# One rope product for each pair of heads, and the odd head's three query items in slots 4, 6 and 8, in a TensorE-bound diffusion block

## The reference

```python
q = (rmsnorm(h @ w_dq, q_norm) @ w_uq).reshape(b, n, N_HEADS, QK_NOPE + QK_ROPE)   # 128 + 64 features a head
qr_l = axial_rope(qr_l, ang_row, ang_col)                  # the 64 rope features of each head are rotated
s = (einsum("bqhd,bkhd->bhqk", q_nope, k_nope)
     + einsum("bqhr,bkr->bhqk", q_rope, k_rope))
p = softmax(s * ATTN_SCALE)
```

## Time and profile before

| what | value |
|---|---|
| median of 3 runs | 2343.84 us |
| lowest and highest of them | 2341.87 and 2344.94 us |
| span of the profiled execution, first to last instruction | 2340.9 us |
| TensorE (PE) busy | 2316.5 us, 99% |
| VectorE (DVE) busy | 1706.3 us, 73% |
| ScalarE (ACT) busy | 807.6 us, 34% |
| GpSimd (POOL) busy | 152.5 us, 7% |
| scores, attention loop and last pass | about 103 to 540 us of the span |
| the odd heads' R products | 123 us, and 230, 338 and 447 us in the loop |

### The profile page before, as it was taken

The page is one execution under the profiler, slowest core; times in us unless marked ns, Lnnn a source line. Parts: engine busy times, 40 slices in busy tenths (PEclk is TensorE's granted clock), DMA queues, the critical chain, the costliest instruction groups (busy, mean ns, idle before and its releaser), DMA issues.

```text
span 2340.9 us, 29301 instructions
## 1 busy us (share of the span) xinstructions
PE 2316.5 (99%) x11037; PEld 1916.2 (82%) x11037; DVE 1706.3 (73%) x2568; ACT 807.6 (34%) x1301; POOL 152.5 (7%) x114
## 2 busy tenths in 40 slices
PE   8999999999999999999999999999999999999998
PEld 5888888888888888888888888888888888888887
DVE  5778788786688888888886764264897777777776
ACT  6355455563443222222223511111532222222224
POOL 0121221100300000000001200000200000000002
PEclk9999999999999999999999999999999999999999
DMA  7101111123112333333332020120111111111112
GB/s 298 34 25 53 43 52 43 43 74 125 64 36 72 108 108 108 108 101 107 108 100 90 19 72 28 45 72 28 45 45 54 46 47 53 54 47 54 54 38 89
DMA packets 49208, 163.35 MB, mean 70 GB/s; under 512 B 5312, under 2 KB 8768, under 8 KB 48960
## 3 DMA queue, kind: packets, MB, share of 16 engines
q1 hardware_dynamic: 49088, 161.72, 20.6%
HBM read 157.51 MB, written 4.19 MB: 69 GB/s over the span
## 4 chain that ended last, share of the span: by engine, by line
PE 94%; DVE 4%; DMA 1%; ACT 0%; issue 0%; SPq 0%; POOL 0%; DVEq 0%; ACTq 0%
PE ps L628 26%; PE ps L630 26%; PE ps L629 26%; PE ps L1106 3%; PE ps L1040 2%; PE ps L1044 2%; PE ps L1042 2%; PE ps L1041 2%; PE ps L1045 2%; PE ps L1085 1%; PE ps L1087 1%; PE ps L1086 1%; DMA ada_ring<-ada_pe 1%; PE ps L876 1%; PE ps L894 0%
## 5 line engine op out<-in xcount | busy, mean ns | idle before, releaser
L2220 DVE SCALAR_TENSOR_TENSOR x<-ps,mods,x 128x512 f32<-128x512 f32 x440 | 322.5, 748 | 145.1 <-PE ps L630 125.6
L628 PE MATMUL ps<-g_hi,w_hi 128*128 128x512 f32 (+1 forms) x848 | 327.5, 386 | 0.1
L630 PE MATMUL ps<-g_hi,w_lo 128*128 128x512 f32 (+1 forms) x848 | 326.5, 385 | 0.0
L629 PE MATMUL ps<-g_lo,w_hi 128*128 128x512 f32 (+1 forms) x848 | 326.5, 385 | 0.0
L628 PE MATMUL ps<-h_hi,op_hi 128*128 128x512 f32 x640 | 249.2, 389 | 0.0
L630 PE MATMUL ps<-h_hi,op_lo 128*128 128x512 f32 x640 | 249.0, 389 | 0.0
L1752 ACT CAST op_hi<-rq 128x512 fp32r<-128x512 f32 x240 | 146.7, 621 | 234.2 <-PE ps L630 228.9
L1763 ACT ACTIVATE g_full<-g_full 128x512 f32<-128x512 f32 x80 | 50.6, 633 | 491.1 <-DVE g_full L2572 491.1
L628 PE MATMUL ps<-h_hi,w_hi 128*128 128x512 f32 x512 | 200.6, 392 | 1.6 <-DVE h_lo L2450 1.5
L630 PE MATMUL ps<-h_hi,w_lo 128*128 128x512 f32 x512 | 199.3, 389 | 0.0
L629 PE MATMUL ps<-h_lo,w_hi 128*128 128x512 f32 x512 | 199.2, 389 | 0.0
(11 more groups left out here) (365 smaller groups left out, 4567.9 us busy)
## 6 DMA issues: line engine op xcount, KB each, us to landing
rq<-stream SPq DMA_DIRECT2D x80, 512.0 KB, 3.6
mod_raw_f<-ada_rows SPq DMA_DIRECT2D x48, 512.0 KB, 3.6
raw<-stream SPq DMA_DIRECT2D x46, 512.0 KB, 4.1
w_lo_f<-stream SPq DMA_DIRECT2D x46, 512.0 KB, 4.4
mod_raw<-ada_rows SPq DMA_DIRECT2D x32, 512.0 KB, 3.5
ada_ring<-ada_pe SPq DMA_DIRECT2D x16, 512.0 KB, 11.4
x<-x_t SPq DMA_DIRECT2D x8, 512.0 KB, 7.4
hraw<-head_w SPq DMA_DIRECT2D x8, 384.0 KB, 3.1
```

Source lines behind the costliest of these rows:

```text
L628: nc.tensor.matmul(out, w[0][wi], a[0][ai], start=start, stop=False)
L629: nc.tensor.matmul(out, w[0][wi], a[1][ai], start=False, stop=False)
L630: return nc.tensor.matmul(out, w[1][wi], a[0][ai], start=False, stop=stop)
L2220: nc.vector.scalar_tensor_tensor(out=x[:, m, HALF[half]], in0=ps[:, out_bank(d, m), :], scalar=mods[:, gate + m:gate + m + 1], in1=x[:, m, ...
```

## The change

The rope weights of the even and the odd head of a pair are put side by side in place of the even head's own twice, so one pair of R items gives the even head's 64 features in rows 0 to 63 and the odd head's in rows 64 to 127. The odd head (`pair_leads` false) has no R items; its W, Q0 and Q1 stand in slots 4, 6 and 8. In `FIRST_ITEMS` the two R items of head 1 are gone. `rope_done` writes the rounded part from and to the head's own rows, and the remainder to the other rows; for the odd head it waits for no rotation, since `qsb` still holds it. For the even head `hraw` arrives in four DMAs: two of them fetch 64 columns (256 bytes) twice a partition, from this head and from the next. For the odd head only the first 384 columns are split by `HW`.

```diff
+FOLLOW_AT = {4: ("W", 0), 6: ("Q", 0), 8: ("Q", 1)}
...
-            if 4 <= k <= 8:
-                kind, half = QUERY_STAGE[k - 4]
-                out.append((kind, gb, half))
+            if pair_leads(gb) and 4 <= k <= 8:
+                out.append((QUERY_STAGE[k - 4][0], gb, QUERY_STAGE[k - 4][1]))
+            if not pair_leads(gb) and k in FOLLOW_AT:
+                out.append((FOLLOW_AT[k][0], gb, FOLLOW_AT[k][1]))
...
+def pair_leads(gb):
+    return head_parity(gb) == 0
...
-                  ("W", -1, 0), ("F", -3, 1), ("M", 0, 3), ("R", -1, 0), ("R", -1, 1), ("X", 0, 3), ("Q", -1, 0),
+                  ("W", -1, 0), ("F", -3, 1), ("M", 0, 3), ("X", 0, 3), ("Q", -1, 0),
...
+        def pair_in(own, other):
+            sp.dma_start(hraw[:, 0:3 * P], own[:, 0:3 * P]).then_inc(in_head, 16)
+            sp.dma_start(rope_of(hraw)[:, :, 0:ROPE], rope_of(own)[:, :, 0:ROPE]).then_inc(in_head, 16)
+            sp.dma_start(rope_of(hraw)[:, :, ROPE:P], rope_of(other)[:, :, ROPE:P]).then_inc(in_head, 16)
+            sp.dma_start(hraw[:, HW:HW + P], own[:, HW:HW + P]).then_inc(in_head, 16)
+            C.add("uv_l")
...
-            C.add("q_rot")
-            dve.wait_ge(q_rot, C.at("q_rot"))
-            q = qr[par]
-            own(nc.vector.tensor_copy(q[:, HALF[k]], qsb[k][:]))
-            low = q[64:128, HALF[k]]
-            last = lo_part(low, qsb[k][64:128, :], low)
+            if par == 0:
+                C.add("q_rot")
+                dve.wait_ge(q_rot, C.at("q_rot"))
+            rows = (slice(0, ROPE), slice(ROPE, P))
+            full, top, low = qsb[k][rows[par], :], qr[par][rows[par], HALF[k]], qr[par][rows[1 - par], HALF[k]]
+            own(nc.vector.tensor_copy(top, full))
+            last = lo_part(low, full, top)
...
+            used = slice(0, HW if pair_leads(gb) else 3 * P)
+            copy(hw_hi[:, used], hraw[:, used]).then_inc(hw_h, 1)
```

More of the change, by code:

```diff
@@ L714, in _, with rope_of @@
         sp.dma_start(tab[:].rearrange("p a t -> p (a t)"), rope).then_inc(in_tab, 16)
+        def rope_of(t):
+            return t[:, 3 * P:HW].rearrange("p (q n) -> p q n", n=P)
+        def pair_in(own, other):
[4 more added lines that the diff above has]
+            C.add("uv_l")
         def head_in(n):
-            sp.wait_ge(uv_l, C.at("uv_l"))
             sp.dma_start(hraw[:], tile_of(head_w, n)).then_inc(in_head, 16)
@@ L727, in _ @@
         sp.wait_ge(pj, 4)
-        sp.dma_start(hraw[:], head_w[0]).then_inc(in_head, 16)
-        C.add("uv_l")
+        pair_in(head_w[0], head_w[1])
         sp.wait_ge(pj, 6)
@@ L734, in _ @@
         C.add("mod_p", 2)
+        sp.wait_ge(uv_l, C.at("uv_l"))
         head_in(1)
@@ L739, in _ @@
             for j in range(2):
-                head_in(i * 2 + (2 + j))
+                if j == 0:
+                    sp.wait_ge(uv_l, C.at("uv_l"))
+                    sp.sem_inc(wait_end, 1)
+                    pair_in(tile_of(head_w, i * 2 + 2), tile_of(head_w, i * 2 + 3))
+                else:
+                    sp.wait_ge(uv_l, C.at("uv_l"))
+                    sp.sem_inc(wait_end, 1)
+                    head_in(i * 2 + 3)
                 for k in range(4):
@@ L1184, in _ @@
         with pe.Fori(0, PASSES) as i:
-            C.enter(i, {"ra": RING_PASS, "rd": RING_PASS - 12, "ex": 16, "q_ready": 2, "hw_l": 2, "uv_l": 2, "ri": 4,
+            C.enter(i, {"ra": RING_PASS, "rd": RING_PASS - 10, "ex": 16, "q_ready": 2, "hw_l": 2, "uv_l": 2, "ri": 4,
                         "ol_l": 4})
@@ L1572, in ring_out @@
                 if k == 0:
-                    C.add("q_ready")
+                    C.add("q_ready", 2)
                 copy(qsb[k][:], ps[:, bank, :]).then_inc(ra, 1)
@@ L1599, in prepare, with head_hi @@
                 split_head(n, half)
-        def head_hi():
-            C.add("in_head", 16)
+        def head_hi(gb):
+            C.add("in_head", 64 if pair_leads(gb) else 16)
             act.wait_ge(in_head, C.at("in_head"))
-            copy(hw_hi[:], hraw[:, 0:HW]).then_inc(hw_h, 1)
+            used = slice(0, HW if pair_leads(gb) else 3 * P)
+            copy(hw_hi[:, used], hraw[:, used]).then_inc(hw_h, 1)
         def value_hi(par):
@@ L1625, in item @@
             elif kind == "HW":
-                head_hi()
+                head_hi(gb)
             elif kind == "UV":
@@ L1702, in _ @@
         with act.Fori(0, passes) as i:
-            C.enter(i, {"rg": RING_PASS, "mx": 16, "in_head": 32, "q_ready": 2, "pv": 40,
+            C.enter(i, {"rg": RING_PASS, "mx": 16, "in_head": 80, "q_ready": 2, "pv": 40,
                         "mod_p": 8, "mod_out": 1})
@@ L2249, in mods_ready, with head_lo @@
             scale_vec(2, mods[:, mod_col(0, SCALE2):mod_col(0, SCALE2) + KD], 1).then_inc(sv_set, 1)
-        def head_lo():
+        def head_lo(gb):
             C.add("hw_h")
             dve.wait_ge(hw_h, C.at("hw_h"))
-            lo_part(hw_lo[:], hraw[:, 0:HW], hw_hi[:]).then_inc(hw_l, 1)
+            used = slice(0, HW if pair_leads(gb) else 3 * P)
+            lo_part(hw_lo[:, used], hraw[:, used], hw_hi[:, used]).then_inc(hw_l, 1)
         def value_lo(par):
@@ L2310, in item @@
             elif kind == "HW":
-                head_lo()
+                head_lo(gb)
             elif kind == "UV":
@@ L2427, in _ @@
         with dve.Fori(0, passes) as i:
-            C.enter(i, {"ra": RING_PASS, "s_mm": 16, "ex": 16, "hw_h": 2, "uv_h": 2, "q_rot": 4, "pv": 40, "ol_r": 4,
+            C.enter(i, {"ra": RING_PASS, "s_mm": 16, "ex": 16, "hw_h": 2, "uv_h": 2, "q_rot": 2, "pv": 40, "ol_r": 4,
                         "v": 16 + 4 + 4 + 6 + 8, "in_mod0": 64, "in_mod1": 64, "mod_out": 1})
@@ L2993, in _ @@
         with pool.Fori(0, passes) as i:
-            C.enter(i, {"q_sh": 4, "gp": 8})
+            C.enter(i, {"q_sh": 2, "gp": 4})
             for gb in range(4):
```

## The result

| | before | after |
|---|---|---|
| median of the first comparison (4 runs each) | 2344.16 us | 2331.07 us |
| median of a second one (9 and 5 runs) | 2342.25 us | 2331.05 us |
| span of the profiled execution | 2340.9 us | 2329.4 us |

The ratio is 0.9946 in the first comparison, 95% interval 0.9933 to 0.9959, and 0.9952 (0.9938 to 0.9965) in the second: faster by 0.5%, 11 to 13 us. The forecast was 9.7 us and 2334.1 us. The measured median lies 0.4 us under the low end of the stated range, 2331.5.

The account below looks back on a forecast made before the run. PE without gaps was taken as the bound: 8.2 us in the loop plus 1.55 before it made 9.7 us, taken from the 2343.84 us median, giving 2334.1 us; range 2331.5 to 2338.3 us.

Parts of the forecast that it names:

- What bounds the kernel: Whole kernel: PE busy 2316.5 of 2340.9 us and without gaps in the loop, so time comes almost only from PE work.
- 2.73 us for a head's R items in the loop: Group 3 of three passes: two R items removed, at six starts of 0.228 us each; 8.2 us in all.
- The walk of group 3: New order on old durations, slots 5 to 8: no PE wait, nearest margin about 0.3 us, at Q1 for T9's `pt_lo`.
- near 26.2: Sign in the loop: group 3 becomes 2.7 us shorter, to near 26.2 us.
- mod_row at 1.22 us, since POOL is idle: Second `mod_row` of group 3 on DVE takes 1.22 us; with 1.94, PE would wait 0.4 us a pass, 1.2 in all.
- Before the loop, 1.55 us instead of 3.0: Head 1's R items: saving held to DVE's idle 1.55 us ahead of the row maximum; bounds nothing and 3.0 us.
- The two remainders do not come sooner with the change: Before the loop, DVE: Q0's and Q1's remainders stay put, since Q0's rounding on ACT stands behind an exponential that does not move.
- relief that is worth nothing: ACT copies, DVE shuffles, POOL operations and the split cut from 640 to 384 columns: beside gapless PE, worth nothing by themselves.
- Rival A: Before the loop nothing is held back: all 3.0 us saved, 11.2 us in all, 2332.7 us; chance 0.10.
- The load, F and the wider operands at nothing: Four-piece load covered (17.7 us for even heads; upper bound 0.6 us for the first), `rope_done` on 64 partitions: no cost.
- `hraw` lands within 5 us: Sign for the head weight loads: `hraw` lands within 5 us.
- Nothing given back behind attention: After attention PE is the chain again and loads are issued by progress, so none of the saving is lost there.

Follow-up runs that it names:

- the products alone, in the loop: Changed kernel with the odd head's twelve rope products put back on PE in each loop pass, result overwritten: 2340.35 us against 2342.56 before, ratio 0.9989.

## Why the prediction was right or wrong

- **What bounds the kernel** was right. PE without gaps is the bound, and taking products off it gave their time back one for one in the loop (the products alone, in the loop).
- **2.73 us for a head's R items in the loop** was right: 2.74, 2.68 and 2.70 us, read from start to start. By the listed 0.39 us each the gain would have been 4.7 us a head.
- **The walk of group 3** was right in its result, no wait, and in the place of the margin. The margin itself was under-sized: 0.3 us forecast, 0.7 measured. Q0's rounding ended 0.18 us earlier than walked. The rest is the walk's: it added listed durations on DVE, while `mod_row` and the `pt_lo` behind it each start 0.08 us before the listed end of the operation ahead. The sign "near 26.2" for group 3 was off too. It was reckoned from a window of 28.90 us, but the group is 30.2 us from OH to OH; the 2.7 us taken off it was right.
- **mod_row at 1.22 us, since POOL is idle,** was right and is shown by making POOL busy. The price of the opposite was forecast as 0.4 us a pass and is 0.14 to 0.2.
- **Before the loop, 1.55 us instead of 3.0,** is the term that was mis-sized: 2.08 us from W on and 2.25 in all. The mechanism, DVE's chain with an idle time that is used up, is shown. But "The two remainders do not come sooner with the change" was wrong: measured from W they were done some 0.5 us sooner. Of this 0.27 us is from the narrower split beside POOL, which I had counted as relief that is worth nothing. The rest is from ACT's pair of roundings, which no longer waits for PE. Rival A, the full 3.0 us, did not come about. The time alone could not have told: 2331.07 us is nearer to rival A's 2332.7 than to the forecast, and it is the place of the stalled T that speaks against A.
- **The load, F and the wider operands at nothing** was right for the load, by experiment. The issue of the pieces takes 1.7 us and not the 1.0 reckoned, and they land in at most 2.4 us. The sign "`hraw` lands within 5 us" failed by its letter, since it did not leave out head 1's single load of 6.6 us. For F no line of the lists of waits shows a cost; it was not varied.
- **Nothing given back behind attention** was right within the scatter of 1.9 us of that stretch.
- **The time.** 9.7 us was the sum; 10.5 us is what the marks show to the end of attention, and 11.2 and 13.1 us what two comparisons of medians show. Of the 0.8 us between the sum and the marks, 0.5 is the error before the loop. The rest is 0.17 us ahead of W and 0.18 in the first pass, which no experiment varied and which are within scatter. The forecast of 2334.1 us was 3.0 us too long, and the measured median lies 0.4 us outside the stated range. About half of the 3.0 us is the value from which the difference was taken: 2343.84 us was the median of three runs, and 2342.2 to 2342.6 us that of later, larger sets. 0.5 us is the term before the loop. The remaining 1.0 us or so stays open; it is of the size of the scatter behind attention. The low end of the range took rival A and the scatter of single runs, and left no room for an error of that starting value.

## What to carry to other kernels

Where a busy PE has no gaps, a removed product is worth its distance to the next start, not its listed duration, and in a steady loop all of it. Ahead of a loop, where engines still hand work to each other one by one, follow the chain of the second engine: it had 1.55 us of idle time, and that, plus what its own links got shorter, was the gain, not the 2.74 us of PE's work. Before such a change is trusted, put the new order on the old durations and look for the nearest margin; here that took a dozen rows and named the one wait that an additional 1.2 us on DVE then produced.

## What the runs showed of the hardware

- POOL's products and `mod_row` hold each other up: 1.22 us alone and 1.88 beside POOL, and POOL's product 1.30 alone and 2.15. A DVE split of weights that was 256 columns narrower made a POOL product beside it 0.27 us shorter (1.89 against 1.62), and this reached PE as 0.27 us, by way of F, a row maximum, an exponential and the remainders behind it.
- A product that starts at the moment of its release holds the next one back by 0.10 us: 0.34 us from its start to the next at Q1 with a wait, 0.24 without.
- The same program's span varies by 1 to 3 us from the start-up and the long stretch after attention. At the start the granted clock fell to 0.50 to 0.58 (means of 2 us) in four of twelve profiled executions. Two microseconds earlier PE had been busy for 1.09 of 2 us, but in the eight others it had been so as well. In the repeat of the changed kernel it stayed there from about 25 to 32 us, and W before the loop was 2.2 us later. The lengths of the loop's groups without an edit in them repeat to 0.1 us over the eleven profiles of the changed kernel and its variants (one group of the kernel before was 0.2 us longer). Differences under 3 us were only to be had from the latter.
